# A two-network fp32 kernel: the first mixer's output end rebuilt, norm roots moved to ScalarE, and gate/up weights landed apart from down weights, three steps ahead

## The reference, cut to what matters

```
def swiglu(h, w1, w3, w2):                    # w1, w3: 1024 x 2752 (2816 in the second block)
    return (silu(h @ w1) * (h @ w3)) @ w2     # gate, up, down
# first block, layer l: m = silu(c) @ w_mod[l] gives shift, scale and gate of every norm
x = x + 0.5 * m[0, 2] * swiglu(adaln_in(x, norm_g[l, 0], m, 0), w1, w3, w2)
mix = mixer(adaln_in(x, norm_g[l, 1], m, 1) @ w_in)
x = x + m[1, 2] * (mix @ w_out)
x = x + 0.5 * m[2, 2] * swiglu(adaln_in(x, norm_g[l, 2], m, 2), ...)
# second block: the same with plain rmsnorm; at the end rmsnorm(h, final_g)
def adaln_in(x, g, m, i):
    return x * rsqrt(mean(x * x) + EPS) * g * (1 + m[i, 1]) + m[i, 0]
```

## Time and profile before

| what | us |
|---|---|
| median of three runs | 1943.57 |
| the profiled execution, its own time | 1947.29 |
| its span, first to last instruction | 1945.5 |
| TensorE matmul busy | 1845.2 |
| VectorE busy | 1414.9 |
| ScalarE busy | 995.3 |
| mean granted TensorE clock | 0.98 |

### The profile page before, as it was taken

The page is one execution under the profiler, slowest core; times in us unless marked ns, Lnnn a source line. Parts: engine busy times, 40 slices in busy tenths (PEclk is TensorE's granted clock), DMA queues, the critical chain, the costliest instruction groups (busy, mean ns, idle before and its releaser), DMA issues.

```text
span 1945.5 us, 38239 instructions
## 1 busy us (share of the span) xinstructions
PE 1845.2 (95%) x16458; PEld 1600.3 (82%) x16458; DVE 1414.9 (73%) x2226; ACT 995.3 (51%) x1618; POOL 6.6 (0%) x15
## 2 busy tenths in 40 slices
PE   2999997999999999999999999999999999999997
PEld 1888786888788887778888888888888888778886
DVE  6889876777788988756667667767667766768664
ACT  3444565544544455444465446456445544566443
POOL 0000000000000000000000000000000000000000
PEclk7999998999999999999999999999999999999999
DMA  8998644676589944446656554355554655424551
GB/s 346 362 365 350 227 176 154 241 273 251 190 344 354 374 173 163 162 157 233 229 184 228 195 196 174 120 200 191 199 205 161 230 209 200 163 98 165 210 207 58
DMA packets 54276, 423.98 MB, mean 218 GB/s; under 512 B 5955, under 2 KB 6131, under 8 KB 26683
## 3 DMA queue, kind: packets, MB, share of 16 engines
q1 hardware_dynamic: 52172, 413.59, 56.3%
q0 software_dynamic: 1936, 7.95, 1.1%
HBM read 420.38 MB, written 1.13 MB: 217 GB/s over the span
## 4 chain that ended last, share of the span: by engine, by line
PE 74%; DVE 14%; ACT 5%; DMA 5%; issue 2%; SPq 0%; DVEq 0%; ACTq 0%
PE pw L421 16%; PE pw L422 15%; PE pw L423 15%; PE acc L421 8%; PE acc L423 8%; PE acc L422 8%; DVE ring_lo L1579 5%; DMA land<-stream 3%; DVE modw L1494 2%; DMA modw<-wmod 1%; PE acc L645 1%; ACT ring_hi L1126 1%; PE pssq L489 1%; PE acc L664 1%; DVE proj L1560 1%
## 5 line engine op out<-in xcount | busy, mean ns | idle before, releaser
L421 PE MATMUL pw<-h_hi,ring_hi 128*128 128x256 bf16 x3224 | 885.7, 275 | 51.4 <-DVE h_lo L1565 36.6
L422 PE MATMUL pw<-h_lo,ring_hi 128*128 128x256 bf16 x3224 | 885.9, 275 | 0.0
L423 PE MATMUL pw<-h_hi,ring_lo 128*128 128x256 bf16 x3224 | 885.4, 275 | 0.0
L1579 DVE TENSOR_TENSOR ring_lo<-land,ring_hi 128x1024 bf16<-128x1024 f32 x633 | 740.6, 1220 | 171.4 <-ACT ring_hi L1126 170.7
L1126 ACT ACTIVATE ring_hi<-land 128x1024 bf16<-128x1024 f32 x633 | 625.1, 1046 | 214.4 <-PE acc L423 104.1
L421 PEld LDWEIGHTS pw<-h_hi,ring_hi 128*128 128x128 bf16 x3224 | 316.6, 98 | 115.9 <-issue 49.6
L421 PE MATMUL acc<-a_hi,ring_hi 128*128 128x256 bf16 x1408 | 383.8, 273 | 1.5 <-DVE a_lo L1627 1.5
L423 PE MATMUL acc<-a_hi,ring_lo 128*128 128x256 bf16 x1408 | 383.8, 273 | 0.0
L422 PE MATMUL acc<-a_lo,ring_hi 128*128 128x256 bf16 x1408 | 383.8, 273 | 0.0
L423 PEld LDWEIGHTS pw<-h_hi,ring_lo 128*128 128x128 bf16 x3224 | 318.1, 99 | 39.1
L422 PEld LDWEIGHTS pw<-h_lo,ring_hi 128*128 128x128 bf16 x3224 | 317.0, 98 | 37.7 <-issue 0.3
(11 more groups left out here) (274 smaller groups left out, 1471.4 us busy)
## 6 DMA issues: line engine op xcount, KB each, us to landing
land<-stream SPq DMA_DIRECT2D x211, 1536.0 KB, 6.5
modw<-wmod SPq DMA_DIRECT2D x144, 512.0 KB, 7.8
biasT<-bias_rows POOLq DMA_DIRECT2D x3, 1536.0 KB, 8.7
biasT<-bias_rows POOLq DMA_DIRECT2D x1, 3072.0 KB, 12.1
cst_s<-cst SPq DMA_DIRECT2D x1, 1792.0 KB, 10.0
x<-xT SPq DMA_DIRECT2D x1, 1024.0 KB, 9.7
out<-proj SPq DMA_DIRECT2D x1, 1024.0 KB, 3.9
par_s<-par SPq DMA_DIRECT2D x1, 699.0 KB, 13.2
```

The lines of the kernel that those rows point to most:

```text
L421: mm(o, lhs[0], rhs[0], start=start, stop=False, skip_group_check=True)
L422: mm(o, lhs[0], rhs[1], start=False, stop=False, skip_group_check=True)
L423: return mm(o, lhs[1], rhs[0], start=False, stop=stop, skip_group_check=True)
L1579: v.tensor_tensor(ring_lo[:, t % RING, b, :], land[:, t % LAND, b, :], ring_hi[:, t % RING, b, :], ALU.subtract).then_inc(lo_ready, 1)
```

## The change

It has six parts.

1. **Landing.** `land` holds two places for gate/up pairs (1 MB each) and `land_d` two for third blocks (512 KB each). `load_triple` becomes `load_pair` and `load_down`, each waiting for its own kind of place. The order of all splits is written out in a list, `SPLITS`. Step j of an ffn splits the down block of step j + 1 and the pair of step j + 3. A pair's ring place is free when `up` of four steps before is done, not its `down`.
2. **End of ab.** `out_part` and `merge_rest` serve ab too, with convolution chunks 4 and 5 between pairs 2 and 3, and chunk 0 after the last turn. VectorE does pair 3's bias ahead of the third convolution chunk.
3. **Roots.** Every root is ScalarE's logarithm and exponential straight from PSUM, with one table set for both. VectorE's mean and reciprocal go, the FFT filter's too.
4. **First step.** `up_first` in every ffn stage.
5. **`wmod` blocks.** 8 of them move from stage 3 to stage 2, and both use 18 steps in place of 20.
6. **Output.** Four DMAs, each after its two chunks.

```diff
-            def load_triple(t, slot):
-                if t >= LAND:
-                    sp.wait_ge(lo_ready, t * 3 - 3 * (LAND - 1))
-                sp.dma_start(land[:, slot]..., stream[t]).then_inc(land_load[slot], 16)
+            def load_pair(t):
+                if t >= LAND:
+                    sp.wait_ge(lo_ready, SPLIT_NO[t - LAND, 1])
+                sp.dma_start(land[:, t % LAND]..., stream[t, :, 0:2 * D]).then_inc(land_load[t % LAND], 16)
+            def load_down(t):
+                n = DOWN_NO[t]
+                if n >= LAND:
+                    sp.wait_ge(lo_ready, SPLIT_NO[DOWN_TRIPLES[n - LAND], 2])
+                sp.dma_start(land_d[:, n % LAND], stream[t, :, 2 * D:3 * D]).then_inc(down_load[n % LAND], 16)
...
                     for g, k in mods[n] if n < len(mods) else []:
                         load_mod(g, k)
-                    if t < NT:
-                        load_triple(t, t % LAND)
+                    load_down(t + 1)
+                    load_pair(t + 3)
...
+                steps[i, j] = [(f + j + 1, 2)] + ([(f + j + 3, 0), (f + j + 3, 1)] if j < NFF - 1 else [])
+        entry.append([(f + 2, 0), (f + 2, 1)] if kind == "ffn" else [(f + 1, 2)])
+        leave[i] = [(after, 0), (after, 1), (after + 1, 0), (after + 1, 1), (after, 2)]
...
+                        if kinds[old] == "ffn" and b < 2:
+                            act.wait_ge(gu_ready, ffn_no[old] * NFF + t - RING - FIRST[old] + 1)
+                        else:
+                            act.wait_ge(triple_used, t - RING + 1)
...
-            def root(what, t):
-                act.wait_ge(recip_ready, ...)
-                fn(t, t, ACT.Sqrt).then_inc(root_ready, 1)
+            def inverse_root(what, dst, src, scale):
+                fn(dst, src, ACT.Ln, scale=scale, bias=eps_col[:, 0:1]).then_inc(ln_done, 1)
+                act.wait_ge(ln_done, ROOT[what])
+                fn(dst, dst, ACT.Exp, scale=-0.5).then_inc(root_ready, 1)
+            def root_table():
+                nc.scalar.preload_act_table_set("natural_log_exp_and_others")
...
-            def reciprocal(dst, src, scale):
-                done(v.tensor_scalar(dst, src, scale, EPS, ALU.mult, ALU.add))
-                v.reciprocal(dst, dst).then_inc(recip_ready, 1)
...
-PART = {"hy": {7: [0], 8: [1, 2], 9: [3]}, "sw": ...}
+PART = {"ab": {4: [4, 5], 5: [0]}, "hy": ..., "sw": ...}
+EARLY = {"ab": [0, 1, 4, 5], "hy": [0, 1, 2, 3], "sw": [0, 1, 2, 3]}
...
-                    if j == 0 and deferred(i):
-                        pe.wait_ge(act_ready, f0)
+                    if j == 0:
+                        if f0:
+                            pe.wait_ge(act_ready, f0)
                         up_first()
...
                 pair_normal(i, "ab", 2)
                 pair_out(i, "ab", 0)
+                pair_bias(i, "ab", 3)
                 gate_conv(i, 2)
-                pair_bias(i, "ab", 3)
-                split_low(t + 5, blocks=(0, 1))
...
-            sp.dma_start(out, h).then_inc(out_saved, 16)
+            for k in range(0, KD, 2):
+                sp.wait_ge(affine_ready, KD * 6 + k + 2)
+                sp.dma_start(out[:, k:k + 2, :], h[:, k:k + 2, :]).then_inc(out_saved, 16)
```

More of the change, by code:

```diff
@@ L79, with split_groups @@
 NT = _n
+def split_groups():
+    entry, steps, own, leave = [], {}, {}, {}
+    for i, (kind, blocks) in enumerate(STAGES):
+        f, after = FIRST[i], FIRST[i] + -(-blocks // 3)
+        entry.append([(f + 2, 0), (f + 2, 1)] if kind == "ffn" else [(f + 1, 2)])
+        if kind == "ffn":
+            for j in range(NFF):
+                steps[i, j] = [(f + j + 1, 2)] + ([(f + j + 3, 0), (f + j + 3, 1)] if j < NFF - 1 else [])
+        else:
+            own[i] = [(t, b) for t in range(f + 2, after) for b in range(3) if 3 * (t - f) + b < blocks]
+            leave[i] = [(after, 0), (after, 1), (after + 1, 0), (after + 1, 1), (after, 2)]
+    return entry, steps, own, leave
+ENTRY, STEPS, OWN, LEAVE = split_groups()
+BEGIN = [(0, 0), (0, 1), (1, 0), (1, 1), (0, 2)]
+SPLITS = list(BEGIN)
+for _i, (_kind, _blocks) in enumerate(STAGES):
+    SPLITS += ENTRY[_i]
+    if _kind == "ffn":
+        for _j in range(NFF):
+            SPLITS += STEPS[_i, _j]
+    else:
+        SPLITS += OWN[_i] + LEAVE[_i]
+SPLITS = [(t, b) for t, b in SPLITS if t < NT]
+SPLIT_NO = {s: n + 1 for n, s in enumerate(SPLITS)}
+DOWN_NO = {t: n for n, t in enumerate(sorted(t for t, b in SPLITS if b == 2))}
+DOWN_TRIPLES = sorted(DOWN_NO)
 def spread(first, last, slots):
@@ L724, in merge_rest @@
                 g = pair_no[i] + len(PAIRS[kind])
-                first = 1 + max(k for ks in PART[kind].values() for k in ks)
+                seen_ks = [k for ks in PART[kind].values() for k in ks]
+                last = PAIRS[kind][-1][-1]
+                low = [k for k in range(KD) if k not in seen_ks and k != last] + [last]
+                high = [k for k in range(KD) if k not in EARLY[kind] and k != last] + [last]
+                pe.wait_ge(pair_o, g - 2)
                 for j in range(4, KD):
-                    out_products(i, j, range(4))
+                    out_products(i, j, EARLY[kind])
@@ new lines, in merge_rest @@
+                if ab:
+                    m.then_inc(triple_used, 1)
+                out_products(i, 3, low, -1, last).then_inc(acc_done, 1)
+                m = out_products(i, 4, high, -1, last)
+                if not ab:
+                    m.then_inc(triple_used, 1)
+                out_products(i, 5, high, -1, last).then_inc(triple_used if ab else acc_done, 1)
+                m = out_products(i, 6, high[0:1], -1, last)
+                if ab:
+                    m.then_inc(acc_done, 1)
@@ L1136, in silu @@
                 fn(a_hi[:, j % (LAG + 1), :], act_in[:, j % 2, :], ACT.Copy).then_inc(a_hi_ready, 1)
-                if j < NFF - 1 and (j or not deferred(i)):
-                    split_high(FIRST[i] + j + AHEAD)
+                if j or not deferred(i):
+                    split_high(STEPS[i, j])
             squares(0)
-            root(("norm", 0), rs[:])
-            split_high(0)
+            root_table()
+            root_of(0)
+            split_high(BEGIN[0:2])
             def pair_exp(i, kind, p):
```

477 lines of the change are left out of this document (227 added, 250 removed).

## The result

The changed kernel took 1911.53 us, median of 4 runs (1910.03 to 1912.69), against 1944.41 (1942.42 to 1946.62) for the kernel before on the same chip: ratio 0.983, 95% interval 0.9813 to 0.9847, so 33 us faster. Its profiled execution has a span of 1910.9 us, 34.6 less than before. The forecast was 1900, with a range of 1886 to 1922.

The account below looks back on a forecast made before the run. The prediction took the kernel to be bound by TensorE's fixed work plus about ten seams. Its terms summed to 45.1 us, of which it kept 43: 1947.3 to 1904, less 3.7 is 1900.5, with a range of 1886 to 1922.

Parts of the forecast that it names:

- The likeliest case: The whole kernel: the seams' gains come about and the time is 1900 us; chance 0.62.
- ab's last part: Sign of being right: no gap over 1 us in mixer ab from the last scores to the projection's end.
- Norm roots and first step: Entries of stages 2, 3 and 5: shorter root chain and `up_first` bring 3.0 us each, 9 in all (5.1 to 11.7).
- Entry of stage 1, end of ab: Stage 1's entry gains 2.5 us (1.0 to 2.7); reordering mixer ab's end gains 8 (4 to 9.1).
- Start, cd, end: Start gains 2.4 us; mixer cd with the entry of stage 5 gains 7; the kernel's end gains 3.2.
- Deferred seams: Seams of stages 5/6, 8/9 and 11: waits for low halves shrink with earlier splits, 4.5 us (2 to 5.2).
- hy: Mixer hy: a landing wait and a table load at its logarithm and exponential shrink, 3 us (1 to 4.9).
- Landing in stage 0: Inside stage 0: splitting pairs a step earlier removes TensorE's short waits for low halves, 2.5 us (0 to 3.5).
- sw: Mixer sw: splits come 3.1 us earlier, the gap falls from 4.0 to 0.9 with its low clock; 6 us (3.1 to 6.5).
- Rival C: Ffn steps: an unlanded down block holds up in-order ScalarE, each step grows, 70 us lost, 1970; chance 0.04.
- A: Seams: clock still falls for 6.7 us and VectorE eats the head start in ab, cd, hy; 26 us gained, 1917; chance 0.24.
- B: Ffn steps of stages 0 and 3: each extra DMA costs transport time, gain shrinks to 19 us, 1925; chance 0.07.

Follow-up runs that it names:

- the kernel with sorted loads: Changed kernel with SyncE's list of loads sorted by the number of the split that frees each load's slot: 1901.61 us, ratio 0.9773.
- roots alone: Kernel before, with only the roots of all norms but the first made one logarithm and one exponential on ScalarE: 1927.96 us, ratio 0.993.
- the pair moved away: Changed kernel with SyncE's loads sorted and stage 0's last pair split at mixer ab's entry: 1895.95 us; without the sorting 1915.97 us.
- two relieved resources: Changed kernel with half the columns of 48 `wmod` blocks multiplied by VectorE, or half loaded by DMA; one profiled execution each: 1905.8 and 1905.1 us.
- both two steps ahead: Changed kernel, loads sorted, pairs and down blocks apart but both split two steps ahead: 1943.98 us; with the down load let through first, 1901.8 us.
- the one with the last `wmod` blocks moved: Changed kernel with SyncE's loads sorted and stage 0's last three `wmod` blocks moved behind `a_lo(21)`: 1897.67 us, ratio 0.9761.

## Why the prediction was right, and where it was not

The likeliest case came about, and the time is 11.5 us above the forecast, 0.6%: 33 us gained for some 43. The mechanism of the seams was right; the forecast is as near as it is also by luck, since terms that were over (5.0) made up for a third of those that were short (15.5). The sum of the terms was 45.1 and the kernel with sorted loads gained 45.0; that it fits so well hides terms that are off in both directions. Of the signs of being right, the one of stage 0 (177 us or less) did not come; ab's last part (0.74), the first product (38.5) and sw's rsT (1.19) did.

*Norm roots and first step.* Right: gap 2.77 for a forecast of 2.9, 3.4 us for 3 at stage 3. Its parts were not: `up_first` gives 0.8 in place of up to 2, the shorter chain 1.8, and the clock the rest. The range's high end, 3.9 an entry, left out the prediction's own case of a clock that does not fall (1.7 + 3.4), and that case came at stage 2. The size left open, what the clock does after 2.8 us, has three answers in these runs: not at all (stage 2), 3.4 us (stages 3 and 5), 6.8 (roots alone, stage 3). The gap's length alone does not settle it.

*Entry of stage 1, end of ab.* 8 for the end, 9.1 and 8.9 measured alone. The roots give another 5.4. Of these 14.5 the change kept 10.6 and the sorted kernel 14.3: the late down blocks took 4.

*Start, cd, end.* 2.5 for 2.4, 7.2 for 7, 3.6 for 3.2. The roots alone made cd slower, so its gain is that of the filter's root and of the moved splits: the roots alone left the filter's square root with a table load of its own. With the splits back at two steps ahead (1914.17) cd kept 6.7 of the 7.2, so the moved splits are worth 0.5 at most.

*Deferred seams.* 6.2 for 4.5 (2.2, 3.2, 0.8), but from another edit than I named: the roots alone give 5.5 of it. In the changed kernel with all splits two steps ahead, though, the two seams are 2.7 longer, so there the step ahead is needed for them. The waits that the term names (1.37, 0.5, the same again, and 0.6 twice) also add up to 4.9, not 5.2.

*hy.* 5.2 for 3. This one is uncertain: the kernel with only ab's end changed was 2.9 us faster in hy too. 1.2 of that is the 1.50 of the earlier trace rows, which is 0.26 there: the splits ahead of the logarithm waited 1.10 us for their landing in place of 2.54. The other 1.7 is a low clock of 3.4 us behind a wait of 1.71 that both have. So a good half of hy's 5.2 may be what differs from execution to execution; that was not tried.

*Landing in stage 0: the step that failed.* "With a pair split a step earlier they go, if VectorE and DMA keep up." The short waits did go, and the condition did not hold: at 0.97 of DMA and 0.9 of VectorE (135.66 of 152 us), the extra pair had to be loaded and split inside the same stage, and TensorE met the arrears in its last step, where nothing covers them: -3.7 in place of 2.5. Less work for either, or (with sorted loads) the pair moved away, brought the stage to 157.1 to 157.4. I had looked at sums of busy time over the stage and never at what stands ahead of the last `a_lo`.

*sw: the other one.* The wait that I counted fell as forecast (1.19, for 0.9), and the low clock moved on to the next wait, 4.48 for a down block: -0.4 in place of 6. I wrote that SyncE "has nothing else to do and waits before each" and took the new issues as free. It is the reverse: because it waits before each, each holds back those behind it.

*Rival C* had this place and mechanism, and gave it 0.04 as a loss of 70 us spread over all steps. It was real, worth 10 us, and sat not in the ffns but in the mixers, where ScalarE's exponential or copy is behind the split. That it can be large shows where the down load stood behind `wmod` loads: 42 us between two kernels that differ in that alone, 37.1 of them in stage 0 and 5.5 in stage 3. *A*, the partial gain, was right in its kind (VectorE eats a head start) for stage 0 only. *B* asked a price for each DMA; with 512 KB and 1024 KB loads queued the changed stage moves 358 GB/s in place of 352, and kernels with as many loads took 157.1 us for the stage, the same as stage 3: no such price is seen.

## What to carry to other kernels

When a load is cut in two, sort the issues on their queue by the moment at which each may start: one that waits for a slot holds back all behind it. Here the sorting brought 9.9 us, and the cut as first made 2.6, which the noise covers. Where an engine may run steps behind another, look at the last step of the stage: arrears are paid there at once, often with half clock behind them, and work that isn't due can go behind the last thing that is. Undo the parts of a change one by one: here the part that gave the change its name had brought 2.6 us, and half of it (three steps ahead) nothing until one pair was moved. And before a few us are put down to an edit, look in the stretches whether they lie where the edit is.

## What the hardware showed that I had not expected

In stage 0, two relieved resources gave the same end to 0.1 us, 214.6 and 214.5, where each alone looked under its limit (VectorE busy 136 of 152 us, DMA 0.97); and a kernel with the same two shares, but without the extra pair, ended the stage without the wait.

The clock behind gaps of 2.8 us stayed up, fell for 3.4 or fell for 6.8 us. Behind gaps of 4.4 us and more inside the stages it fell for 6.8, but for one of 5.14 (roots alone, mixer ab), with 3.4, and one of 7.12 (both two steps ahead, 1943.98, stage 0), with 10.2. Neither the gap nor TensorE's work ahead of it settles this. In hy TensorE waits 2.05 us for `mskb` in the kernel with sorted loads and in the one with the last `wmod` blocks moved, with the same TensorE instructions before it. The windows begin 1.3 us after that wait in each; the clock is the last but two, 0.50 and 1.00, and it is worth 1.6 us:

```profile
1242.50:1245.80 3.30, 3.30 (x34) 3.30 (x33) 2.60 (x10) 1.73 (x8) 0.00 (x0) 0.50 0.79 251
```

```profile
1239.80:1243.10 3.30, 3.30 (x55) 3.05 (x55) 2.64 (x10) 1.68 (x8) 0.00 (x0) 1.00 0.73 226
```
